# Experts of a hybrid trunk: fp32 products taken as three fp32r passes, with low parts made by VectorE

## The reference

```python
def moe(h, w_router, b_router, w_gu, w_down):
    scores = jax.nn.sigmoid(h @ w_router)
    sel_g = (scores + b_router).reshape(..., 4, 4)       # 16 experts in 4 groups
    best = argmax(top_k(sel_g, 2).sum(-1))               # one group for each token
    combine = ...                                        # top 2 experts of that group, weights normalised
    gate, up = split(einsum('ld,edf->lef', xs, w_gu), 2) # w_gu: 16 x 1024 x 512
    hid = silu(gate) * up * cw[..., None]                # 256 wide for each expert
    return einsum('lef,efd->ld', hid, w_down)            # w_down: 16 x 256 x 1024
```

## Time and profile before

| | |
|---|---|
| median of three runs | 2851.33 us |
| the profiled execution's own time | 2844.31 us |
| its span | 2842.5 us |
| TensorE busy, all stages | 2559.0 us, 90% |
| VectorE, GpSimd, ScalarE busy | 51%, 28%, 26% |
| expert steps of layer 0 | 382.0 to 652.0, 270.0 us |
| expert steps of layer 1 | 1169.2 to 1438.0, 268.8 us |
| expert steps of layer 2 | 1940.6 to 2209.0, 268.4 us |
| expert steps of layer 3 | 2544.7 to 2797.6, 252.9 us |

### The profile page before, as it was taken

The page is one execution under the profiler, slowest core; times in us unless marked ns, Lnnn a source line. Parts: engine busy times, 40 slices in busy tenths (PEclk is TensorE's granted clock), DMA queues, the critical chain, the costliest instruction groups (busy, mean ns, idle before and its releaser), DMA issues.

```text
span 2842.5 us, 30129 instructions
## 1 busy us (share of the span) xinstructions
PE 2559.0 (90%) x11915; PEld 1877.4 (66%) x11915; DVE 1454.2 (51%) x1956; ACT 753.1 (26%) x1265; POOL 803.5 (28%) x429
## 2 busy tenths in 40 slices
PE   5789999998988879999988967789999799989997
PEld 3789854446877778644468957685445699864444
DVE  6866643335746677433456489773333426640013
ACT  1223221003554442200033344421010333130111
POOL 3547300003543432000026479710000347500000
PEclk6899899998999998999989988879999899979999
DMA  7734659990321146499915410155989133538880
GB/s 267 246 108 122 206 188 348 344 347 31 109 87 60 60 126 215 168 338 343 354 39 170 133 36 22 33 178 214 348 326 338 60 105 104 152 123 300 298 297 36
DMA packets 291851, 524.41 MB, mean 184 GB/s; under 512 B 9472, under 2 KB 141056, under 8 KB 291328
## 3 DMA queue, kind: packets, MB, share of 16 engines
q1 hardware_dynamic: 288256, 519.33, 51.9%
q10 hardware_dynamic: 3456, 3.15, 0.3%
HBM read 517.73 MB, written 4.72 MB: 184 GB/s over the span
## 4 chain that ended last, share of the span: by engine, by line
PE 70%; DVE 12%; ACT 4%; issue 3%; DMA 2%; POOL 2%; ACTq 0%; SPq 0%; DVEq 0%
PE ps L1924 23%; PE ps L1941 12%; PE ps L1661 6%; PE ps L1662 5%; PE ps L1663 5%; PE ps L1729 2%; DVE uw L1352 2%; PE ps L1862 1%; PE ps L1886 1%; DVE macc L2017 1%; PE ps L1887 1%; POOL wlo L1591 1%; PE ps L1763 1%; PE ps L1962 1%; PE ps L1963 1%
## 5 line engine op out<-in xcount | busy, mean ns | idle before, releaser
L1591 POOL TENSOR_TENSOR wlo<-ring,whi 128x1024 fp32r<-128x1024 f32 x202 | 535.2, 2666 | 1428.6 <-ACT whi L1458 1428.6
L1924 PE MATMUL ps<-ring,xg 128*128 128x512 f32 x1536 | 702.8, 595 | 0.0
L1924 PEld LDWEIGHTS ps<-ring,xg 128*128 128x128 f32 x1536 | 280.9, 191 | 296.3 <-issue 296.0
L2017 DVE SCALAR_TENSOR_TENSOR macc<-ring,cond_s,macc 128x1024 f32<-128x1024 f32 x280 | 387.1, 1441 | 4.8 <-DMA ring<-w_mod 4.8
L2241 DVE SCALAR_TENSOR_TENSOR hid<-ps,cws,sg 128x256 f32<-128x256 f32 x96 | 46.4, 484 | 652.6 <-ACT sg L1552 652.6
L1941 PE MATMUL ps<-ring,hidt 128*128 128x512 f32 x768 | 351.2, 601 | 2.3 <-ACT hidt L1527 2.3
L1661 PE MATMUL ps<-hh,whi 128*128 128x384 f32 x840 | 302.8, 360 | 33.3 <-POOL wlo L1591 20.6
L1662 PE MATMUL ps<-hl,whi 128*128 128x384 f32 x840 | 290.8, 346 | 0.0
L1663 PE MATMUL ps<-hh,wlo 128*128 128x384 f32 x840 | 290.4, 346 | 0.0
L1458 ACT ACTIVATE whi<-ring 128x1024 fp32r<-128x1024 f32 x202 | 207.0, 1054 | 278.2 <-DMA ring<-gmlp_w_out 82.7
L1941 PEld LDWEIGHTS ps<-ring,hidt 128*128 128x128 f32 x768 | 147.1, 193 | 183.4 <-issue 183.4
(11 more groups left out here) (366 smaller groups left out, 4193.4 us busy)
## 6 DMA issues: line engine op xcount, KB each, us to landing
ring<-moe_w_gu SPq DMA_DIRECT2D x192, 1024.0 KB, 8.0
ring<-w_mod SPq DMA_DIRECT2D x96, 1024.0 KB, 8.3
ring<-moe_w_down SPq DMA_DIRECT2D x96, 1024.0 KB, 6.2
ring<-gmlp_w_in SPq DMA_DIRECT2D x32, 1024.0 KB, 6.3
ring<-ssd_w_in SPq DMA_DIRECT2D x21, 1024.0 KB, 5.3
ring<-hgrn_w_in SPq DMA_DIRECT2D x20, 1024.0 KB, 5.2
ring<-gmlp_w_out SPq DMA_DIRECT2D x16, 1024.0 KB, 6.8
ring<-ssd_w_out SPq DMA_DIRECT2D x8, 1024.0 KB, 5.9
```

The costliest lines, as they stand in the source:

```text
L1591: pool.tensor_tensor(split_sub(wlo, s0), raw_sub(s0), split_sub(whi, s0).bitcast(F32), ALU.subtract).then_inc(S["lo_ready"], 1)
L1924: ins = pe.matmul(ps[:, s % 2, :], xg[:, w, k, :], whole(what, s, 4)[:, k % 4, :], start=(k == 0), stop=(k == KD - 1))
L2017: ins = dve.scalar_tensor_tensor(out=acc[:, v, :], in0=w[:, k, :], scalar=by, in1=acc[:, v, :], op0=ALU.mult, op1=ALU.add)
```

## The change

`SPLIT` names the chunks that are split in each layer: A and B in layers 0 to 2; A, B and D in layer 3. For these:

- ScalarE makes a high part of each half chunk in `whi` (1024 columns), VectorE the low part, written over the raw weights in the ring (`ring_lo` lies on `ring`). `wlo` and GpSimd are not used. Each product becomes three fp32r passes of 128x512.
- The ring of the experts has six slots (`SIX`): 0 to 3, 6 and 7, since `whi` is in use. A chunk takes the slot of the sixth before it. It is free when TensorE has done both halves (for M, when VectorE has done its four operations).
- The gathered tokens become `xgh` (ScalarE) and `xgl` (VectorE, 16 subtractions from PSUM between the routing's steps). The gather's banks are free only when xgl is written.
- In layer 3 the turned hidden tile gets a low part as well (`hidden_rest` by VectorE).
- The hidden tile's turn comes behind the second gate and up product, not the sixth. `window_low` comes one step later.
- In layers 0 to 2 the four modulation operations of a step are placed between the low parts: in steps 0, 6, 12 and 18 all four behind `hid`, in the other steps with a chunk one ahead of low A0, one ahead of low A1 and two behind `hid`.

In the diff, `TURNED` is layer 3 and `mixed` holds in layers 0 to 2.

```diff
+SPLIT = {0: 'AB', 1: 'AB', 2: 'AB', 3: 'ABD'}
+SIX, OPS_AT = 6, (0, 4, 8, 8, 12, 16, 16)
...
-            part(("mod", l + 1) if what == "M" else (l, what), 1, 0 if what == "M" else -1, True)
+            rows_of = 0 if what == "M" else -1 if what not in SPLIT.get(l, "") else 2 if what == "D" else 4
+            part(("mod", l + 1) if what == "M" else (l, what), 1, rows_of, SIX if l in SPLIT else RING)
...
+        ring_lo = at("ring_lo", [P, RING, 2 * SUB], F32R, place[0])
+        xgh = ar("xgh", [P, NW, KD, P], F32R, 48)
+        xgl = at("xgl", [P, NW, KD, P], F32R, hoff)
...
 # ScalarE, experts
+                ahead = lambda what, i: feed(sb((l, what), i) + 3) if what in SPLIT.get(l, "") and i >= 0 and (l in TURNED or i < 2 * STEPS - 2 or (what, i) == ("A", 2 * STEPS - 2)) else None
                 for s in range(STEPS):
+                    ahead("A", 2 * s)
+                    ahead("A", 2 * s + 1)
                     if s:
                         hidden_over(s - 1)
-                    act.wait_ge(S["moe_used"], used[places[l, "B"][s]])
+                    ahead("B", 2 * s)
+                    ahead("B", 2 * s + 1)
+                    expert_used(act, l, "B", s)
                     if s >= 2:
                         act.wait_ge(S["hid_ready"], n0 + s - 1)
                     act.activation(sg[:, s % 2, :], ps[:, s % 2, 0:DE], ACT.Silu).then_inc(S["sg_ready"], 1)
+                    ahead("D", 2 * s - 2)
+                    ahead("D", 2 * s - 1)
                     if s and s % EG == 0:
                         window_high(s // EG - 1)
...
 # TensorE, experts
+                def wide_product(out, xhi, xlo, s0, half, first, last):
+                    hi = whi[:, nth[s0] % SPL, 512 * half:512 * half + 512]
+                    lo = low_part(s0)[:, 512 * half:512 * half + 512]
+                    pe.matmul(out, xhi, hi, start=first, stop=False)
+                    pe.matmul(out, xhi, lo, start=False, stop=False)
+                    return pe.matmul(out, xlo, hi, start=False, stop=last)
...
+                        if l in SPLIT:
+                            s0 = sb((l, what), 2 * s + k // 2 % 2)
+                            if k % 2 == 0:
+                                low_in(s0)
+                            ins = wide_product(ps[:, s % 2, :], xgh[:, w, k, :], xgl[:, w, k, :], s0, k % 2, k == 0, k == KD - 1)
+                            if k % 2:
+                                ins.then_inc(S["sub_done"], 1)
+                            if s and k == 1:
+                                hidden_over(s - 1)
...
 # VectorE
+            def low(l, what, i):
+                s0 = sb((l, what), i)
+                n = nth[s0]
+                dve.wait_ge(S["hi_ready"], n + 1)
+                out = low_part(s0).rearrange("p (k n) -> p k n", k=chunk_rows[s0 // 2] // 2)
+                dve.tensor_tensor(out, raw_sub(s0), split_sub(whi, s0).bitcast(F32), ALU.subtract).then_inc(S["low_ready"], 1)
...
                 for s in range(STEPS):
+                    if l in TURNED:
+                        low(l, "B", 2 * s + 1)
+                        if s:
+                            low(l, "D", 2 * s - 2)
+                            hidden_rest(s - 1)
+                            low(l, "D", 2 * s - 1)
+                        ahead("A", 2 * s + 2)
+                    if mixed:
+                        cut = 0 if s % SIX == 0 or not mods else 2
+                        if cut:
+                            mod_ops(l, s, 0, 1)
+                        ahead("A", 2 * s + 2)
+                        if cut:
+                            mod_ops(l, s, 1, 2)
+                        ahead("A", 2 * s + 3)
+                        ahead("B", 2 * s + 2)
                     dve.wait_ge(S["sg_ready"], n0 + s + 1)
...
-                    if s and e == 0:
+                    if s and e == (1 if l in SPLIT else 0) and s >= EG:
                         window_low(w - 1)
...
+                    if l in TURNED:
+                        ahead("A", 2 * s + 3)
+                        ahead("B", 2 * s + 2)
+                    if mixed:
+                        if mods:
+                            mod_ops(l, s, cut, 4)
+                        ahead("B", 2 * s + 3)
```

More of the change, by code:

```diff
@@ L128, in stream_plan @@
         for what, _ in moe_order(l):
-            part(("mod", l + 1) if what == "M" else (l, what), 1, 0 if what == "M" else -1, True)
+            rows_of = 0 if what == "M" else -1 if what not in SPLIT.get(l, "") else 2 if what == "D" else 4
+            part(("mod", l + 1) if what == "M" else (l, what), 1, rows_of, SIX if l in SPLIT else RING)
     return places, rows, ring_slots(wide)
 def ring_slots(wide):
-    slots, fills, before, held, count, narrow, i = [], [], [], {}, [0] * RING, 0, 0
+    slots, fills, before, runs, held, count, narrow, i = [], [], [], [], {}, [0] * RING, 0, 0
     for c, w in enumerate(wide):
         i = i + 1 if w and c and wide[c - 1] else 0
-        s = i % RING if w else narrow % RAW
+        s = i % w if w else narrow % RAW
         if w and s < RAW:
             s = (narrow + s) % RAW
+        elif w == SIX:
+            s += RING - SIX
         if not w:
@@ L147, in ring_slots @@
         fills.append(count[s])
-        before.append(held.get(s) if s < RAW or i >= RING else None)
+        before.append(held.get(s) if s < RAW or i >= w else None)
+        runs.append(c - i)
         held[s] = c
-    return slots, fills, before
+    return slots, fills, before, runs
 def out_mods(l, c, outs):
@@ L186, in trunk @@
     used = {c: n + 1 for n, c in enumerate(whole_at)}
+    vector_lows, pool_lows = [0], [0]
+    for s in order_of:
+        by_vector = chunk_rows[s // 2] in (2, 4)
+        vector_lows.append(vector_lows[-1] + by_vector)
+        pool_lows.append(pool_lows[-1] + (not by_vector))
     ctx = ExitStack()
@@ L511, in sb, with expert_used @@
             return 2 * part[j // 2] + j % 2 if j < 2 * len(part) else 2 * part[-1] + 2 + j - 2 * len(part)
+        def expert_used(eng, l, what, s):
+            if what in SPLIT.get(l, ""):
+                eng.wait_ge(S["sub_done"], nth[sb((l, what), 2 * s + 1)] + 1)
+            else:
+                eng.wait_ge(S["moe_used"], used[places[l, what][s]])
         def end_of_experts(l):
@@ L1462, in feed @@
                 first = min(upto - SPL + 1, NSUB)
-                while fed[0] <= min(nth[first] + SPL - 1, nth[NSUB] - 1) and order_of[fed[0]] // 2 < first // 2 + RAW:
+                while fed[0] <= min(nth[first] + SPL - 1, nth[NSUB] - 1) and order_of[fed[0]] // 2 < first // 2 + (SIX if in_experts(first) else RAW):
                     high(fed[0])
@@ L2006, in mod_chunk @@
                     held = max((g for g in range(group) if acc_of(g) is acc_of(group) and g not in PE_GROUPS), default=None)
-                    if held is not None:
+                    if held is not None and 0 in parts:
                         dve.wait_ge(S["mod_summed"], held + 1)
@@ L2011, in mod_chunk @@
                     for v in range(2):
+                        if 2 * k + v not in parts:
+                            continue
                         by = cond[:, 2 * q + k, v:v + 1]
@@ L2146, in route @@
                 pairs = rt[:, 2:4, :, :].rearrange("p a t e -> p (a t e)")[:, 0:72].rearrange("p (g e) -> p g e", e=6)
+                if l in SPLIT:
+                    low(l, "A", 0)
+                    low(l, "A", 1)
                 dve.wait_ge(S["route_ready"], l + 1)
```

138 lines of the change are left out of this document (100 added, 38 removed).

## The result

The kernel after takes 2917.64 us (median of four runs, 2912.51 to 2922.86) against 2851.26 for the kernel before on the same chip: ratio 1.024, interval 1.0228 to 1.0252. It is slower by 66 us; I had forecast 89 us faster. The profiled execution's span is 2916.1 us, its own time 2917.85.

A forecast was written before the change was run, and what follows sets the result against it. TensorE's issue was taken to bound the expert stretches; 3 x (31.3 - 15 - 0.5) + (47 - 5) = 89.4 us saved gave 2754.9, or 2762 us against the median shown; range 2738 to 2812, the forecast's own 2740 to 2785.

The forecast's parts named there:

- The product: Expert stretches: three fp32r passes take 0.695 us, 0.163 less than an fp32 product; 31.3 us saved per layer 0-2, 47.0 in layer 3.
- The low part: VectorE in the expert steps: one 128x1024 subtraction in SBUF takes 1.15 us, bounds 1.1 and 1.32.
- Layer 3: Expert stretch without modulation chunks: 47 us gained less 5 for stalls, start and end, leaving 42 us.
- The signs that I had named against the forecast: TensorE idle over 25 us a layer, or clock under 0.97, would make the forecast wrong toward B, C or D.
- The gather: Sixteen subtractions of gathered rows go into idle VectorE time in route; 0.5 us a layer counted, bounds 0 and 2.
- stalls (b): Layers 0 to 2: A in a modulation chunk's slot lands late, ScalarE waits ahead of hidden tile's copy; 10 us a layer.
- Part (a): Layers 0 to 2, steps after a window's end: VectorE's low parts come late for TensorE; 5 us a layer.
- D: Rival, layers 0 to 2: each of 16 late-freed modulation chunks exposes a 4.7 us landing; 75 us a layer, 2941; chance 0.06.
- C: Rival: TensorE's gaps drop its clock to 1.2 GHz; eight gaps cost 16 us a layer, 2810 us total; chance 0.08.
- B: Rival, layers 0 to 2: transfers bind at 2.87 us a MiB; only 7 us a layer gained, 2790 total; chance 0.22.

## Why the prediction was wrong

**What held.** TensorE's issue was the bound before. The product: passes 0.232 us apart, steps of 9.23 us for 9.21. The low part: 1.22 us for 1.15, within its bounds. Layer 3: 44.4 us less where the sum had 42; its stalls came to 208.5 - 205.9 = 2.6 us, not 5. The signs that I had named against the forecast both came: TensorE idle for more than 25 us a layer (46.0) and a clock under 0.97 (0.92).

**The gather.** Between router and experts layer 0 took 2.6 us more than before, where I counted 0.5. That is the clock, not the subtractions. TensorE's timeline and window at the gather's start in the kernel after, for the earlier trace rows, and then the timeline of the version with the later turn, whose stretch from gather to experts took 389.4 - 370.1 = 19.3 us against 19.5 before and 22.0 after:

```profile
...
367.75 0.76 PE L1929 MATMUL ps<-spread,thi 128*128 128x512 f32 x1 [3.32 <-DVE tlo L2328]
368.32 0.63 PE L1930 MATMUL ps<-spread,tlo 128*128 128x512 f32 x1
...
```
```profile
...
367.70:373.40 5.70, 5.64 (x16) 4.75 (x17) 3.76 (x11) 0.98 (x2) 0.00 (x0) 0.50 0.00 0
...
```
```profile
...
370.06 0.47 PE L1929 MATMUL ps<-spread,thi 128*128 128x512 f32 x1 [3.62 <-DVE tlo L2328]
...
```

The 16 subtractions are hidden. In layers 1 to 3 the same stretch did not grow either (21.0, 22.2 and 22.0 us before, 20.8, 21.9 and 21.9 after). Layer 0's router also begins 5 us later (349 for 344 us); that start varies between 344 and some 352 in the kernels of this study, in a stage which none of them changes, and I have no cause for it.

**The step that failed: stalls (b).** It had the place right (an A that takes a modulation chunk's slot, ScalarE standing at it, the hidden tile's copy queued behind) and put 10 us a layer on it. Measured in layer 0: 38.1 us of idle time before down products, plus some 21 us of slow clock (262.5 busy against 241.2 where the gaps are gone). Part (a), low parts late for TensorE, came to 5.6 us where I had 5, but partly by luck: 3.1 us stand in steps 10, 13 and 22, which I had named, and 2.5 in steps 1, 2 and 7. Five things were missing from (b):

- I followed the waits once, from a step that starts on time. The late A comes back: it delays high part, low part, the two modulation operations behind it and the slot of the next chunk. Step 9's M was free 16.8 us after the step's start (495.56), where I had 13.4. I had computed one turn of a loop.
- I excused the steps behind 0, 6, 12 and 18 as covered by the column sums. In step 6 VectorE does all four operations behind `hid`, and its M was as late as the others: step 7 lost 4.3 us of idleness before its down product and 3.0 of clock, the most of all. Steps 7, 13 and 19 together have 12.0 of the 38.1 us.
- I took a slot that goes to a B as harmless, with 5 us to spare, and looked only at the B. But SyncE's queue is in order: while B9 waited for M7's slot, M9, D8 and A10 stood behind it. Steps 3, 9, 15 and 21, which I had not listed, have 10.4 of the 38.1 us. Only 15.2 us stand where I looked, in steps 4, 10, 16 and 22, for my 10.
- A landing was put at 4.7 us, as from an empty queue. Here it took 5.3 at least and 8.3 in the middle. The earlier trace rows is layer 3's; the trace of the kernel before had the longer time in the very stretch in question. For its layer 0:

```profile
...
DMA to landing us min/median/max: 4.8/8.7/13.9
...
```

  The run with few bytes for M prices the queue at up to 47 us over three layers.
- The clock. It cost 1.6 to 3.0 us behind each of nine gaps, as said above. I had taken as proof that it would hold through such waits. The two windows cut one wait in two: TensorE stood still for 3.62 us, from 358.92 to 362.54, and the clock held. TensorE's timeline before:

```profile
...
362.54 0.48 PE L1886 MATMUL ps<-spread,thi 128*128 128x512 f32 x1 [3.62 <-DVE tlo L2217]
...
```

  That was one outcome of two. Behind layer 0's same wait (2.65 to 3.63 us long) the clock was at 0.50, or fell to it within 2.5 us, in 11 of the 14 profiles, and stayed at 1.00 in three. One row was no proof.

"TensorE: Matmul & The Clock Gate" of the Trainium skill ("HAM oscillation") says that gaps from waiting on transfers throttle the clock again; this trace agrees, at 0.50 behind gaps of 4.32 us, and it is the rule which I had set aside. But the gaps were made by the order, and went with it.

**The rivals.** D was the one that came true in layers 0 to 2, and I gave it 0.06. Its price, one landing of 4.7 us for each of 16 chunks, gave 314 us a layer (270 + 75 - 31); measured 308.5, 310.0, 301.7. It came out by other terms: 11 gaps of 2 to 4.5 us before the down product, and the clock; that the time comes near its price is luck. I had set against it that half of the slots go to a B or a D that has 5 us to spare. D loaded ahead of M shows that the users make the difference (104 us), but in the order of this change seven of the 16 slots go to an A, and a B that takes one of the others holds up the A behind it in the queue. C, the clock, had 16 us a layer for eight gaps; some 19 behind nine long ones in layer 0 (and the rest of the 21 elsewhere) is its mechanism, but as a follower of D's. B, the transfers as the bound, falls: DMA's share went down from 0.87 to 0.78. (Its price had 12 us in it, 250 + 12, which its text does not derive; nothing here hangs on them.) But the rate I used was too good. Where the full queue bound most, the windows show 357 to 362 GB/s at a share of 0.96 to 0.97 (about 370 at a share of 1, an estimate, so 2.8 us a MiB instead of 2.65). "DMA: Bandwidth & Descriptors" of the Trainium skill (its table of ceilings) has about 358 for one core; that is near to this rate, though layer 2 of the run with narrow operations and both orders held 362 over 247 us.

**How sure.** Shown, by changing one thing each: order on VectorE (130 us), the order of loading (104), VectorE's load (111), the bytes (47), ScalarE's order (4, not told from none), six slots by themselves (7). Those numbers do not add up to the loss, and need not if each cuts the same loop somewhere, as the timelines suggest. Not shown: how the loss divides between the late slots that go to an A and those that hold up the queue; and what the slow clock would cost without the gaps, since no run has one without the other. The 21 us are a difference between two profiles.

## What to carry to other kernels

Where an in-order engine frees a buffer behind work that waits for a transfer, and the freed buffer is for the transfer which the same engines want next, follow the waits through at least two periods with the late arrival put back in at the top; a stall priced on one turn that starts on time is a lower bound. Where the queue that asks for transfers is in order too, look also at what stands behind each request that waits. Put what frees a slot ahead of what waits for data, or give the late slot to a chunk that is wanted late: with the work unchanged either was worth over 100 us here. When a large cut of the bounding engine's time is planned, check each step that is excused from a rival's mechanism; here an excused one lost the most.

## What was not expected of the hardware

- Under load, with several MiB asked for ahead, a transfer took 8.3 us in the middle and 10.7 at most from issue to landing, against 4.7 at the least in layer 3.
- TensorE's granted clock after an idle gap is not given by the gap's length. In layer 0 it was 1.00 behind 2.11 us and 0.50 behind 4.32 us, but in layer 2 a gap of 1.91 us was followed by a slow down product and one of 3.11 us was not. In layer 0's gather a wait of 3.62 us was followed by 1.00 for 5.7 us in one profile and one of 3.32 us by 0.50, which alone is 2.6 us of difference between two profiles.
- With the copy of the hidden tile moved, 17.7 us less of TensorE's busy time in three layers came with 11.1 us more of its idle time, in one profile of each kernel.
